# Up product in seven-product form, up and down as two phases

## The reference

```
z = h @ w_in;  oA = windowed attention(z), oB = forgetting attention(z)
h = LN1(alpha*h + concat(oA, oB) @ w_o)          # alpha = 2 ** 0.25
h = LN2(alpha*h + relu(h @ w_up)**2 @ w_down)    # w_up 2048 x 8192, w_down 8192 x 2048
y = h + sigmoid(h @ w_pg + b_pg) * (p @ w_pe)
```

## Time and profile before

| | |
|---|---|
| median of 3 runs | 3007.03 us (3004.54 to 3007.76) |
| span of the profiled execution, first to last instruction | 2998.6 us |
| the profiled execution's own total | not shown on the page; the runs' median is 8.4 us more than the span |
| TensorE busy | 2830.7 us, 20869 matmuls |
| VectorE, ScalarE, POOL busy | 1283.9, 854.8, 310.6 us |
| granted TensorE clock, mean | 0.985 of full speed |
| DMA | 230.71 MB, 77 GB/s over the span |

### The profile page before, as it was taken

How to read it: one execution, slowest core, us unless ns; L and a number is a source line. 1 busy time by engine, 2 the same in 40 slices (tenths; PEclk the granted TensorE clock), 3 DMA queues, 4 the chain that set the end, 5 groups by cost and what they waited for, 6 DMA issues and landing times.

```text
span 2998.6 us, 51516 instructions
## 1 busy us (share of the span) xinstructions
PE 2830.7 (94%) x20869; PEld 2751.4 (92%) x20869; DVE 1283.9 (43%) x1694; ACT 854.8 (29%) x1361; POOL 310.6 (10%) x305
## 2 busy tenths in 40 slices
PE   1889999999999979999999999999999999998898
PEld 0868899999889979999999999999999999998898
DVE  8654434334453384333333333333333333346732
ACT  3534434334332253112211211221122122214521
POOL 6210012112211140000000000000000000004200
PEclk8989999999999989999999999999999999999999
DMA  3201122222212222222222222222222222221231
GB/s 121 75 28 35 40 82 78 80 77 77 69 50 84 84 64 78 79 85 80 83 78 86 84 85 83 80 79 84 85 78 84 79 85 85 85 74 61 83 119 52
DMA packets 65270, 230.71 MB, mean 77 GB/s; under 512 B 9280, under 2 KB 10176, under 8 KB 64576
## 3 DMA queue, kind: packets, MB, share of 16 engines
q1 hardware_dynamic: 57312, 211.31, 22.0%
q0 software_dynamic: 6160, 15.41, 1.6%
q10 hardware_dynamic: 1616, 1.18, 0.1%
HBM read 217.71 MB, written 10.16 MB: 76 GB/s over the span
## 4 chain that ended last, share of the span: by engine, by line
PE 62%; DVE 2%; issue 1%; ACT 0%; POOL 0%; POOLq 0%; ACTq 0%; DVEq 0%
PE tile L342 60%; PE misc L342 1%; DVE acc L1013 0%; DVE x_lo L1019 0%; DVE w_lo L971 0%; DVE acc L1245 0%; DVE st L1000 0%; DVE st L1002 0%; DVE acc L1009 0%; ACT st L951 0%; DVE st L987 0%; DVE acc L981 0%; PE misc L403 0%; DVE st L998 0%; DVE st L1275 0%
## 5 line engine op out<-in xcount | busy, mean ns | idle before, releaser
L342 PE MATMUL tile<-x_hi,w_hi 128*128 128x288 f32 (+1 forms) x4000 | 885.3, 303 | 44.9 <-DVE x_lo L1019 22.2
L342 PE MATMUL tile<-x_lo,w_hi 128*128 128x288 f32 (+1 forms) x4000 | 859.5, 297 | 0.0
L342 PE MATMUL tile<-x_hi,w_lo 128*128 128x288 f32 (+1 forms) x4000 | 858.8, 296 | 0.0
L342 PEld LDWEIGHTS tile<-x_hi,w_hi 128*128 128x128 f32 (+1 forms) x4000 | 641.4, 189 | 74.4 <-issue 67.1
L342 PEld LDWEIGHTS tile<-x_lo,w_hi 128*128 128x128 f32 (+1 forms) x4000 | 645.5, 189 | 1.2
L342 PEld LDWEIGHTS tile<-x_hi,w_lo 128*128 128x128 f32 (+1 forms) x4000 | 645.1, 189 | 1.3
L665 ACT ACTIVATE w_hi<-w_raw 128x1024 fp32r<-128x1024 f32 x394 | 406.2, 1052 | 635.7 <-PE tile L342 617.6
L971 DVE TENSOR_TENSOR w_lo<-w_raw,w_hi 128x1024 fp32r<-128x1024 f32 x394 | 483.1, 1243 | 208.5 <-ACT w_hi L665 208.4
L342 PE MATMUL tile<-hid_hi,w_hi 128*128 128x288 f32 x2048 | 439.2, 296 | 3.9 <-DVE acc L1245 3.8
L342 PE MATMUL tile<-hid_lo,w_hi 128*128 128x288 f32 x2048 | 438.5, 296 | 0.0
L342 PE MATMUL tile<-hid_hi,w_lo 128*128 128x288 f32 x2048 | 438.3, 296 | 0.0
(11 more groups left out here) (197 smaller groups left out, 2079.1 us busy)
## 6 DMA issues: line engine op xcount, KB each, us to landing
w_raw<-in_w SPq DMA_DIRECT2D x394, 512.0 KB, 3.6
acc<-in_x SPq DMA_DIRECT2D x4, 1152.0 KB, 9.4
out_y<-st POOLq DMA_DIRECT2D x16, 288.0 KB, 2.7
out_fox_v<-v_t POOLq DMA_DIRECT2D x8, 288.0 KB, 2.6
out_fox_k<-k_t POOLq DMA_DIRECT2D x8, 288.0 KB, 2.4
c_t<-in_ck POOLq DMA_DIRECT2D x8, 256.0 KB, 3.0
c_v<-in_cv POOLq DMA_DIRECT2D x8, 256.0 KB, 2.9
p_raw<-in_p POOLq DMA_DIRECT2D x1, 576.0 KB, 4.2
```

The costliest lines, as they stand in the source:

```text
L342: ins = nc.tensor.matmul(dst[:, h, :], w, x[:, h * HALF:(h + 1) * HALF], start=first and a == 0, stop=last and a == 2)
```

## The change

A product of two up tiles (2 x 128 hidden features) with 2048 features of h is taken as a 2 x 2 product of blocks: weights A (tile by half of the features), x side B (half of the features by half of the tokens). The first two blocks of hidden features (8 tiles) stay as they were. The other 28 pairs of tiles use seven products of 8 feature tiles x 288 columns x 3 parts. The sums of the x side are made once (`t_sums`, in `acc`, split into `t_hi`, `t_lo`); four sums of the weight side are made per pair on VectorE (`sum_of`). The seven products go to three banks per pair, two sets of banks alternate; ScalarE saves three intermediate values (`snap`), VectorE makes three of the four blocks of the result (`combine`), ScalarE takes relu and square (`finish_block`), POOL stores each block in DRAM (`save_block`). Two pairs of weights are held raw and split in 15 buffers of 128x1024. The hi parts go through five places, four of them in parts of `x_hi` and `x_lo` that the products don't read.

Down comes after all of up, block by block: POOL loads the hidden tiles back (`hid_back`), ScalarE and VectorE split them (`hid_high`, `hid_low`), into the halves of `x_hi` and `x_lo` in turn. h is stored in DRAM before its sums overwrite it and loaded back into `acc` ahead of the first residual, which now scales it by alpha.

```diff
+FAST = 28
+PRODUCTS = 7
+A11, A12, S2, S1, S3, S4, A22 = range(PRODUCTS)
+FREED = (3, 4, 5, 7)
+X_SIDE = ((False, 0, 0), (False, 8, 0), (True, 8, 1), (True, 0, 0), (True, 0, 1), (False, 8, 1), (True, 8, 0))
+        BANKS = ((misc[:, 0:HALF], misc[:, 512:512 + HALF], misc[:, 1024:1024 + HALF]),
+                 (misc[:, 1536:1536 + HALF], tiles_ps[0][:, 0, 0:HALF], tiles_ps[0][:, 1, 0:HALF]))
...
 SP
+            with sp.Fori(0, FAST // 2 - 1) as i:
+                for q in range(2):
+                    sp.wait_ge(product_done, lin(PROD_0 + PRODUCTS * q + 2, i, 2 * PRODUCTS))
+                    block_in(q, A11, i * 16 + (W_UP + 16 + 4 * q))
+                    block_in(q, A12, i * 16 + (W_UP + 16 + 4 * q + 1))
+                    sp.wait_ge(product_done, lin(PROD_0 + PRODUCTS * q + 7, i, 2 * PRODUCTS))
+                    block_in(q, S3, i * 16 + (W_UP + 16 + 4 * q + 2))
+                    block_in(q, A22, i * 16 + (W_UP + 16 + 4 * q + 3))
+            for j in range(8):
+                if j < RING:
+                    sp.wait_ge(product_done, PROD_0 + PRODUCTS * LAST + FREED[j])
+                fetch_from(U_D + j, (U_D + j) % RING, W_DOWN + j)
...
 TensorE
+            def fast_pair(p, i=None, dp=0, last=False):
+                q = p % 2
+                e, a, c = BANKS[q]
+                banks = (e, a, e, c, e, c, e)
+                pe.wait_ge(combined, lin(COMB_0 + 3 * (p - 1), i, 3 * dp))
+                pe.wait_ge(relu_done, lin(STD_UP + 4 * (p - 1), i, 4 * dp))
+                for r in range(PRODUCTS):
+                    pe.wait_ge(a_ready, lin(PRODUCTS * p + r + 1, i, PRODUCTS * dp))
+                    if r == 2:
+                        pe.wait_ge(snapped, lin(3 * p + 1, i, 3 * dp))
+                    if r == 4:
+                        pe.wait_ge(snapped, lin(3 * p + 2, i, 3 * dp))
+                    if r == 5:
+                        pe.wait_ge(snapped, lin(3 * p + 3, i, 3 * dp))
+                    if r == 6:
+                        pe.wait_ge(combined, lin(COMB_0 + 3 * p + 2, i, 3 * dp))
+                    diff, row, half = X_SIDE[r]
+                    xh, xl = (t_hi, t_lo) if diff else (x_hi, x_lo)
+                    cols_ = slice(HALF * half, HALF * half + HALF)
+                    for k in range(8):
+                        hi = hi_weights(q, r, k, last)
+                        lo = a_lo[:, SETS[q][r], 128 * k:128 * k + 128]
+                        for n, (w, x) in enumerate(((hi, xh), (hi, xl), (lo, xh))):
+                            ins = nc.tensor.matmul(banks[r], w, x[:, row + k, cols_],
+                                                   start=r in (0, 1, 3) and k == 0 and n == 0, stop=k == 7 and n == 2,
...
+            quad(T_MLP, U_MLP, 2)
+            for k in range(4):
+                tile(T_MLP + 4 + k, U_MLP + 8 + 2 * k, after=T_MLP + k if k < 2 else T_MLP + 2 + k)
+            pe.wait_ge(t_ready, 4)
+            with pe.Fori(0, FAST // 2 - 1) as i:
+                for q in range(2):
+                    fast_pair(q, i, 2)
+            fast_pair(LAST - 1)
+            fast_pair(LAST, last=True)
+            down(0)
+            with pe.Fori(0, FF_BLOCKS // 2 - 1) as i:
+                for j in range(2):
+                    down(1 + j, i)
...
 ScalarE
+            def high(p, r, i=None, dp=0, last=False):
...
+                    act.wait_ge(product_done, lin(PROD_0 + PRODUCTS * p + r - 3, i, PRODUCTS * dp))
+                copy(hi_view(q, r, last), by_256(raw(q, r))).then_inc(a_hi_done, 1)
+            def snap(p, k, i=None, dp=0):
+                e, a, c = BANKS[p % 2]
+                dst, bank, r = ((P1_COPY, e, 0), (U2_COPY, e, 2), (P5_COPY, c, 3))[k]
+                act.wait_ge(product_done, lin(PROD_0 + PRODUCTS * p + r + 1, i, PRODUCTS * dp))
+                copy(dst, bank).then_inc(snapped, 1)
+            def fast_pair(p, i=None, dp=0, last=False):
+                n = p + 1
+                high(p, S1, i, dp, last)
+                snap(p, 0, i, dp)
+                high(p, S3, i, dp, last)
+                if last:
+                    hid_high(0, first=1)
+                finish_block(p, 0, i, dp)
+                high(p, S4, i, dp, last)
+                snap(p, 1, i, dp)
+                high(p, A22, i, dp, last)
+                snap(p, 2, i, dp)
+                if last:
+                    hid_high(1, first=1)
+                    ahead.upto(U_D)
+                    hid_high(2, first=1)
+                    ahead.upto(U_D + 1)
+                else:
+                    high(n, A11, i, dp, n == LAST)
+                    high(n, A12, i, dp, n == LAST)
+                finish_block(p, 1, i, dp)
+                hid_high(3, first=1) if last else high(n, S2, i, dp, n == LAST)
+                finish_block(p, 2, i, dp)
+                finish_block(p, 3, i, dp)
+            act.wait_ge(units_begun, 3 + U_D)
+            for k in range(4):
+                act.wait_ge(block_saved[k], SAVED_0)
+            for r in (A11, A12, S2):
+                high(0, r)
...
 VectorE
+            def fast_pair(p, i=None, dp=0, last=False):
+                n = p + 1
+                low(p, S2, i, dp, last)
+                low(p, S1, i, dp, last)
+                combine(p, 0, i, dp)
+                low(p, S3, i, dp, last)
+                hid_low(0) if last else sum_of(n, S1, i, dp)
+                low(p, S4, i, dp, last)
+                if not last:
+                    sum_of(n, S2, i, dp)
+                low(p, A22, i, dp, last)
...
+                combine(p, 1, i, dp)
...
+                    sum_of(n, S3, i, dp)
+                    low(n, A11, i, dp, n == LAST)
+                combine(p, 2, i, dp)
...
+                    sum_of(n, S4, i, dp)
+                    low(n, A12, i, dp, n == LAST)
+            def down(b, i=None, db=0):
                 for k in range(KT):
+                    ahead.upto(U_D + 8 * b + k // 2 + 2, i, 8 * db)
+                    n = T_D + 16 * b + k
+                    if b == 0:
+                        dve.wait_ge(h_back[k // 4], 16)
...
+                    if k % 4 == 1:
+                        hid_low(4 * b + 4 + k // 4, i, db)
...
 POOL
+            for k in range(4):
+                pool.wait_ge(ln_h, KT + 4 * k + 4)
+                pool.dma_start(h_saved_d[4 * k:4 * k + 4].rearrange("k p t -> p k t"), acc[:, 4 * k:4 * k + 4, :]).then_inc(h_saved, 16)
...
+            hid_back(0)
+            hid_back(1)
+            for k in range(4):
+                save_block(LAST, k)
+                if k < 2:
+                    hid_back(2 + k)
+            pool.wait_ge(product_done, PROD_0 + PRODUCTS * FAST)
+            for k in range(4):
+                pool.dma_start(acc[:, 4 * k:4 * k + 4, :], h_saved_d[4 * k:4 * k + 4].rearrange("k p t -> p k t")).then_inc(h_back[k], 16)
+            for m in range(4, 8):
+                hid_back(m)
             pool.dma_start(p_raw[:, :, :], t["p"]).then_inc(p_landed, 16)
```

More of the change, by code:

```diff
@@ L335, in _ @@
+            with sp.Fori(0, (UNITS - U_PE + 8) // RING) as i:
+                for j in range(RING):
+                    fetch_from(i * RING + (U_PE - 8 + j), (U_PE - 8 + j) % RING, i * RING + (W_LAST + j))
         @block.tensor
@@ L346, in products, with tile @@
                 return ins
[L348 to L350 removed]
+            def tile(n, u, i=None, dn=0, du=0, x_gen=None, between=None, c0=0, after=None):
+                wait_freed(pe, n - 2 if after is None else after, i, dn)
                 for c in range(KT):
@@ L917, in _, with t_high @@
+            def t_high(k, row, half):
+                act.wait_ge(t_sum, 4)
+                copy(quarter(t_hi, row, half), quarter(acc, row, half)).then_inc(t_hi_done, 1)
             act.wait_ge(x_ready, 2 + 3 * KT)
             ahead.upto(U_MLP + 9)
-            up(T_MLP, U_MLP, 0)
+            for k in range(4):
+                hidden(k)
+            for k, (row, half) in enumerate(((8, 1), (0, 0), (0, 1), (8, 0))):
+                ahead.upto(min(U_MLP + 11 + 2 * k, U_D - 1))
+                t_high(k, row, half)
+                hidden(4 + k)
@@ new lines, in _ @@
+            act.wait_ge(units_begun, 3 + U_D)
[3 more added lines that the diff above has]
+                high(0, r)
+            with act.Fori(0, FAST // 2 - 1) as i:
+                for q in range(2):
+                    fast_pair(q, i, 2)
+            fast_pair(LAST - 1)
+            fast_pair(LAST, last=True)
+            def down(b, i=None, db=0):
+                for k in range(8):
+                    ahead.upto(U_D + 8 * b + k + 2, i, 8 * db)
+                    if k % 2 == 0:
+                        hid_high(4 * b + 4 + k // 2, i, db, 2 if b == 0 else 0)
@@ new lines, in sum_of @@
+            def sum_of(p, r, i=None, dp=0):
+                q = p % 2
+                first, second, op, needs = {S1: (S3, A22, ALU.add, (S3, A22)), S2: (S1, A11, ALU.subtract, (A11,)),
```

(16 more changed lines are left out.)

381 lines of the change are left out of this document (285 added, 96 removed).

## The result

The changed kernel takes **2915.21 us** (median of 4 runs, 2914.9 to 2917.41) against 3005.78 us before: ratio 0.9701, 95% interval 0.9687 to 0.9714. The sign held, and so did the main mechanism, fewer matmuls on TensorE's path; the time lies 17 us under the 2932 forecast and 3 us under the range.

The account below looks back on a forecast made before the run. TensorE's matmuls bound the up and down stage; -89.7 - 2.8 + 7.1 + 8.1 + 4.0 - 1.6 = -74.9 us takes the span from 2998.6 to 2923.7, and with 8.4 us to the median the forecast is 2932 us, range 2918 to 2964.

Parts of the forecast that it names:

- The sign: Whole kernel: the change makes it faster, chance 0.94; same 0.01, slower 0.05.
- the main mechanism: Up pairs: 28 pairs save 24 matmuls each, 672 on TensorE's path at 133.5 ns, -89.7 us.
- The number of matmuls times their distance: Up and down products: the time is matmuls times 133.5 ns, plus whatever keeps TensorE idle.
- The pair's steady state: Inside the fast up pairs: ScalarE 11.8 and VectorE 15.0 us fit under TensorE's 22.4 us, nothing late, 0 per pair.
- The quad's gap: Quad's end, ahead of the standard up tiles: the 2.8 us wait for the third relu goes, -2.8 us.
- The stall ahead of the first product: From standard tiles into fast pairs: the first split waits behind the last standard tile's store, +7.1 us, bounds 5.5 to 9.
- The three stalls in down: From fast pairs into down: late fourth hidden tile, h's return and next tiles' refill, 0.9 + 1.2 + 6.0, together +8.1 us.
- The down loop has 768, nearest to 833: 6 x 1.2 = 7.2: Down loop's back edges: six gaps of 1.2 us, by the nearest loop's matmul count; all loop gaps together change -1.6 us.
- This holds if a matmul of the new form keeps its 133.5 ns: Fast pairs' products: matmuls adding into one bank keep their distance, costed 0; upper bound 0.05 us more on each.
- the 8.4 us between span and the runs' median stay: Whole kernel: the runs' median stays 8.4 us above the profiled span, so a span of 2923.7 gives 2932 us.
- the clock: Behind the two long stalls, at the first product and in down: half clock loses 1.4 to 2.5 us each, +4.0 us.

Follow-up runs that it names:

- experiment 8: Changed kernel with ScalarE's first fast splits ahead of its last standard tile's work, without waiting there for the standard blocks' stores: 2906.09 us, ratio 0.9666.
- Experiment 9: Changed kernel with POOL's queue reordered in the last pair, so hidden tiles and half of h are loaded earlier: 2901.52 us, ratio 0.9648.
- experiment 2: Changed kernel with an unused buffer of 128 bytes per partition ahead of the weight buffers: 2915.41 us, ratio 0.9702.
- experiment 11: Changed kernel with all down blocks' hidden tiles in the upper token half and 128 bytes ahead of the weight buffers: 2908.88 us, ratio 0.9687.
- experiment 6: Changed kernel with 192 satisfied waits on TensorE ahead of the quad, moving the later loops' code 192 instructions further on: 2945.74 us, one run.
- experiment 1: Changed kernel with the 24 matmuls of each pair's last product issued twice: 3028.98 us, ratio 1.0081.

## Why the prediction was right, and where it failed

**Right.** The number of matmuls times their distance is the time of this stage: -89.6 measured, and an eighth product costs its 24 x 132.2 ns 28 times. The pair's steady state was free: no wait inside a pair, though VectorE got 219 us more to do. The quad's gap went. The stall ahead of the first product was the chain named (6.9 for 7.1), as experiment 8 shows by taking the chain away. The three stalls in down were the ones named, by tile and cause; in the sum 8.9 for 8.1, with the first larger (2.1 for 0.9), the second too (3.7 for 1.2) and the third half as large (3.2 for 6.0). That the sum comes so close is luck. The first part of h landed 9.4 us after its issue, where the prediction took the shortest of the earlier trace rows, 5.4; that made the second stall larger, and it and the half clock brought TensorE later to the third. Experiment 9 shows that the cause of the three stalls is the order on POOL's queue.

**Failed: "The down loop has 768, nearest to 833: 6 x 1.2 = 7.2".** It measured 0. The step took a gap's price from the size of the body alone, by the nearest row. Size is not it: the down loop's body of 1588 instructions has no gap where the changed kernel has it, nor 256 later, nor behind the longer pair loops, and gaps of 2.6 to 3.1 us between starts at one place (192 later).

**Failed: "This holds if a matmul of the new form keeps its 133.5 ns".** It was costed at nothing on one side only: the bound asked whether the new form could be slower. It was 1.18 ns faster in the pairs and 0.8 in down, 10.4 us over 10848 matmuls. Shown for down (experiments 2 and 11): 131.67 ns where weights and columns agree modulo 256 bytes, 133.33 where not. In the pairs the cause is open: there the distances are 131.1 to 133.1 ns by product, and they move with the pad of experiment 2, so addresses have a part in them, but the two values of the down blocks don't describe them. Nor are addresses all: in experiments 8 and 11 a whole stage went at 130.0 ns in one execution and at 133.3 in others with the same matmuls at the same addresses.

**Failed: "the 8.4 us between span and the runs' median stay".** It became 2.1. In every later run whose profiled execution has its own time, that time is 1.6 to 2.0 us above the span (2915.05 over 2913.1; 3005.6 over 3004.0). For the kernel before it is 1.5 to 1.7. So the profiled execution of before took about 3000.2, some 3 us under the lowest of its four timed runs: the 8.4 were mostly the difference between that execution and the others, not a fixed part.

**Too small: the clock.** 4.0 costed, 8.8 measured. I charged the two long stalls only and let 2.8 us of idle be free, as the earlier trace rows and the next matmuls of before show it. But three stalls in 25 us, the first of only 2.1, each left TensorE at a granted 0.50 afterwards.

The sum: -7.2 (gaps) - 10.4 (distance) - 6.3 (span to median), against +4.8 (clock), +0.6 (stalls) and +1.4 outside the stage, is the 17 us.

## What to carry to other kernels

Ask of each bound "below nothing too": the distance of a matmul is worth looking up per loop, and a pad of 128 bytes is worth a try (4.9 us in down here). Look it up in more than one execution, for a whole stage can go at another distance. Cost the back edge of a long loop by its code's length and place, not by the nearest loop, and try a shift of the code before changing the loop. At a change of phase, look at what stands behind the last stores on each queue: two such orders cost 22 us here.

## What the runs showed of the hardware

- A loop's code that is moved by 192 instructions cost TensorE 26 us in six turns, moved by 256 nothing. In experiment 6, at three turns a gap of 2.6 to 2.7 us between starts is followed after 15 matmuls by one of 1.1 to 1.4, at three a gap of 2.8 to 3.1 us by half clock (starts 0.24 us apart). The trace names another engine's last work as the releaser of such a gap.
- In the down loop a 288-column matmul goes out every 131.67 or 133.33 ns by how the addresses of weights and columns lie to each other modulo 256 bytes (experiments 2 and 11). This is no rule for all loops: the pairs have 131.1 to 133.1 ns by product, and in two executions one stage went at 130.0 ns throughout (experiments 8 and 11). What decides that is open.
- 2.07 us of idle left TensorE at a granted clock of 0.50 at the start of down; the gaps of 2.2 and 2.3 us at the down loop's first back edge (experiments 1 and 6) did not, the starts behind them being 0.13 us apart. At other back edges of these two runs 2.1 to 2.9 us did, so the length of the idle time alone doesn't decide it. What does is open.
- A satisfied wait costs TensorE about 0.05 us: 128 more of them, two to an instruction, made an idle time 6.9 us longer.
